# Meta tokens' squares load 16 columns, norm rows and key factors spread with all 128 rows, first attention's meta outputs four heads at once

## The reference

```
def rms_norm(x, g):
    y = xf * lax.rsqrt(jnp.mean(xf * xf, axis=-1, keepdims=True) + EPS)
    return (y * g.astype(jnp.float32)).astype(x.dtype)

# first attention: 8 query heads, 2 key and value heads of 128
q = rms_norm(q.reshape(B, Tp, N_HEADS, A_HEAD_DIM), gq)
k = rms_norm(k.reshape(B, Tp, A_KV_HEADS, A_HEAD_DIM), gk)
o = jnp.einsum('bqgrk,bqkgd->bqgrd', p, vsel)        # four query heads share one value head

# second attention: two maps of 8 heads of 64
q1 = rms_norm(q1.reshape(B, Tp, N_HEADS, B_HEAD_DIM), gq)
k1 = rms_norm(k1.reshape(B, Tp, N_HEADS, B_HEAD_DIM), kn_b)
```

## Time and profile before

| | |
|---|---|
| median of 3 runs | 1302.97 us (1302.85 to 1303.08) |
| span of the profiled execution, first to last instruction | 1300.2 us |
| what the median lies above that span | 2.8 us |
| TensorE matmuls busy | 1276.4 us, 98% |
| TensorE weight loads busy | 1183.3 us, 91% |
| VectorE busy | 980.0 us, 75% |
| ScalarE busy | 669.6 us, 51% |
| GpSimd busy | 494.2 us, 38% |

### The profile page before, as it was taken

How to read it: one execution, slowest core, us unless ns; L and a number is a source line. 1 busy time by engine, 2 the same in 40 slices (tenths; PEclk the granted TensorE clock), 3 DMA queues, 4 the chain that set the end, 5 groups by cost and what they waited for, 6 DMA issues and landing times.

```text
span 1300.2 us, 27004 instructions
## 1 busy us (share of the span) xinstructions
PE 1276.4 (98%) x8914; PEld 1183.3 (91%) x8914; DVE 980.0 (75%) x1567; ACT 669.6 (51%) x1103; POOL 494.2 (38%) x454
## 2 busy tenths in 40 slices
PE   8999999999999999999999999999999999999998
PEld 7999999999999989999888898888888988888887
DVE  5686899975656668999765687799866776999553
ACT  5545555554455555666544354455444565455442
POOL 1142455541212216555411033289611102799222
PEclk9999999999999999999999999999999999999999
DMA  8731556665633315666567555666666543666762
GB/s 218 156 98 50 155 170 180 175 176 165 183 110 110 102 34 166 191 189 182 163 196 235 156 166 159 187 186 191 197 193 190 147 136 89 179 193 189 204 190 82
DMA packets 403203, 209.20 MB, mean 161 GB/s; under 512 B 20552, under 2 KB 397680, under 8 KB 403104
## 3 DMA queue, kind: packets, MB, share of 16 engines
q1 hardware_dynamic: 402016, 205.37, 55.1%
q0 software_dynamic: 784, 2.51, 0.9%
q10 hardware_dynamic: 320, 0.21, 0.1%
HBM read 206.98 MB, written 1.27 MB: 160 GB/s over the span
## 4 chain that ended last, share of the span: by engine, by line
PE 90%; DVE 6%; issue 2%; POOL 1%; ACT 1%; DMA 0%; DVEq 0%; POOLq 0%; ACTq 0%
PE bank L621 22%; PE bank L615 15%; PE bank L617 14%; PE bank L616 14%; PE bank L622 12%; DVE w_lo L2083 2%; PE bank L764 1%; PE bank L1186 1%; PE bank L1188 1%; PE bank L1187 1%; PE bank L751 1%; PE bank L723 1%; PE bank L1038 1%; PE bank L1025 1%; PE bank L693 1%
## 5 line engine op out<-in xcount | busy, mean ns | idle before, releaser
L2083 DVE TENSOR_TENSOR w_lo<-w_raw,w_hi 128x1024 fp32r<-128x1024 f32 x391 | 514.6, 1329 | 28.7 <-ACT w_hi L1443 27.9
L1443 ACT ACTIVATE w_hi<-w_raw 128x1024 fp32r<-128x1024 f32 x391 | 410.6, 1052 | 130.8 <-PE bank L622 66.4
L615 PE MATMUL bank<-split_x,w_lo 128*128 128x272 f32 (+2 forms) x1128 | 329.2, 292 | 0.2 <-issue 0.2
L617 PE MATMUL bank<-split_x,w_hi 128*128 128x272 f32 (+2 forms) x1128 | 322.8, 286 | 0.0
L616 PE MATMUL bank<-split_x,w_hi 128*128 128x272 f32 (+2 forms) x1128 | 322.7, 286 | 0.0
L621 PE MATMUL bank<-split_w,w_hi 128*128 128x512 f32 x880 | 306.9, 392 | 0.7 <-POOL split_w L1942 0.5
L622 PE MATMUL bank<-split_w,w_lo 128*128 128x256 f32 x880 | 246.5, 280 | 0.0
L615 PEld LDWEIGHTS bank<-split_x,w_lo 128*128 128x128 f32 x1128 | 212.4, 188 | 2.8 <-issue 0.6
L616 PEld LDWEIGHTS bank<-split_x,w_hi 128*128 128x128 f32 x1128 | 212.5, 188 | 0.3
L617 PEld LDWEIGHTS bank<-split_x,w_hi 128*128 128x128 f32 x1128 | 212.4, 188 | 0.3
L621 PEld LDWEIGHTS bank<-split_w,w_hi 128*128 128x128 f32 x880 | 164.7, 187 | 37.8 <-POOL split_w L1942 0.8
(11 more groups left out here) (300 smaller groups left out, 1854.5 us busy)
## 6 DMA issues: line engine op xcount, KB each, us to landing
w_raw<-in_mlp_w_dram SPq DMA_DIRECT2D x256, 256.0 KB, 3.2
w_raw<-in_w_up_dram SPq DMA_DIRECT2D x176, 256.0 KB, 3.3
w_raw<-in_w_down_dram SPq DMA_DIRECT2D x64, 256.0 KB, 3.2
w_raw<-in_a_w_in_dram SPq DMA_DIRECT2D x64, 256.0 KB, 3.4
w_raw<-in_w_in_a_dram SPq DMA_DIRECT2D x32, 256.0 KB, 4.1
w_raw<-in_w_kv_b_dram SPq DMA_DIRECT2D x32, 256.0 KB, 3.2
w_raw<-in_a_w_out_dram SPq DMA_DIRECT2D x32, 256.0 KB, 3.2
w_raw<-in_w_down_dram SPq DMA_DIRECT2D x32, 192.0 KB, 3.8
```

Source lines behind the costliest of these rows:

```text
L615: pe.matmul(dst, lo, mov_h, start=first, stop=False)
L617: return pe.matmul(dst, hi, mov_h, start=False, stop=last)
L1443: act.activation(w_hi[:, n % R, :], w_raw[:, n % R, :], ACT.Copy)\
L2083: dve.tensor_tensor(w_lo[:, n % R, :], w_raw[:, n % R, :], w_hi[:, n % R, :].bitcast(F32), ALU.subtract)\
```

## The change

1. Sums of squares: for M only the 16 meta tokens' columns are loaded, and 16 rows of the sums are written. The two key heads of the first attention keep the 128 columns (`every_row`).
2. Spreads: for M all 128 rows of the factor's column are used with the first 16 columns of the identity. The tile of the array becomes 128 by 128 in `spread` and 128 by 64 in `spread_key`.
3. `meta_outputs` of the first attention makes two matmuls of 64 columns in place of eight of 16, since four heads share a value head. The second attention's stays.
4. VectorE: the factor buffer `fq_a` is set to 1.0 once at the start, and `query_sums` adds for M on 16 rows in place of 128.

```
             def spread(dst, column, tiles, off=0):
                 for tt in tiles:
                     lo, hi = TOK[tt]
-                    n = hi - lo
-                    ins = pe.matmul(dst[:, lo - off:hi - off],
-                                    column(tt)[0:n, :].to_broadcast([n, P]),
-                                    ident[0:n, 0:n], start=True, stop=True)
+                    ins = pe.matmul(dst[:, lo - off:hi - off], column(tt).to_broadcast([P, P]),
+                                    ident[:, 0:hi - lo], start=True, stop=True)
...
-            def head_squares(r0, slot, two, ssq_sem, sums=misc[2]):
+            def head_squares(r0, slot, ssq_sem, sums=misc[2], every_row=False):
...
-                    ins = pe.matmul(dst, u_ring[:, slot, lo:lo + P], rhs, start=True, stop=True)
+                    lo, hi = TOK[tt]
+                    n = P if every_row else hi - lo
+                    ins = pe.matmul(sums[0:n, 3 * r0 + TT[tt]:3 * r0 + TT[tt] + 1],
+                                    u_ring[:, slot, lo:lo + n], ones[:, 0:1], start=True, stop=True)
...
             def meta_outputs(att, v_of):
...
-                for hh in range(H):
-                    prob, val = pt_m[0:META, hh, :], v_of(hh, "M")[0:META, :]
-                    ins = pe.matmul(dst[:, META * hh:META * (hh + 1)], val, prob,
+                n = 4 if att.name == "a" else 1
+                for hh in range(0, H, n):
+                    prob, val = pt_m[0:META, hh:hh + n, :], v_of(hh, "M")[0:META, :]
+                    ins = pe.matmul(dst[:, META * hh:META * (hh + n)], val, prob,
                                     start=True, stop=True)
...
@@ spread_key
-                                        fac(fk_a, 2 * c + e, TT[tt])[0:n, :].to_broadcast([n, 64]),
-                                        ident[0:n, 0:n], start=True, stop=True)
+                                        fac(fk_a, 2 * c + e, TT[tt]).to_broadcast([P, 64]),
+                                        ident[:, 0:hi - lo], start=True, stop=True)
@@ squares_sums
-                    ins = pe.matmul(SUM_B[:, c0 + TT[tt]:c0 + TT[tt] + 4:3], sq_b[n % 2][:, lo:lo + P],
-                                    headcol, start=True, stop=True)
+                    ins = pe.matmul(SUM_B[0:hi - lo, c0 + TT[tt]:c0 + TT[tt] + 4:3],
+                                    sq_b[n % 2][:, lo:hi], headcol, start=True, stop=True)
...
+            dve.memset(fq_a, 1.0)
```

More of the change, by code:

```diff
@@ L701, in rb_sums @@
                     .then_inc(S["rb_sums"], 1)
-            def head_squares(r0, slot, two, ssq_sem, sums=misc[2]):
+            def head_squares(r0, slot, ssq_sem, sums=misc[2], every_row=False):
                 for tt in "ABM":
-                    lo = TOK[tt][0]
-                    if two:
-                        dst = sums[:, 3 * r0 + TT[tt]:3 * r0 + TT[tt] + 4:3]
-                        rhs = headcol
-                    else:
-                        dst = sums[:, 3 * r0 + TT[tt]:3 * r0 + TT[tt] + 1]
-                        rhs = ones[:, 0:1]
-                    ins = pe.matmul(dst, u_ring[:, slot, lo:lo + P], rhs, start=True, stop=True)
+                    lo, hi = TOK[tt]
+                    n = P if every_row else hi - lo
+                    ins = pe.matmul(sums[0:n, 3 * r0 + TT[tt]:3 * r0 + TT[tt] + 1],
+                                    u_ring[:, slot, lo:lo + n], ones[:, 0:1], start=True, stop=True)
                 ins.then_inc(ssq_sem, 1)
@@ L888, in _ @@
                         pe.wait_ge(a_sq, k + 1)
-                        head_squares(8 + k, k % 4, False, a_ssq)
+                        head_squares(8 + k, k % 4, a_ssq, every_row=True)
                 if g == 13:
@@ L915, in last_squares_a @@
                 pe.wait_ge(a_sq, 10)
-                head_squares(7, 9 % 4, False, a_ssq, misc[3])
+                head_squares(7, 9 % 4, a_ssq, misc[3])
                 pe.wait_ge(S["tile_read"], ST["in"].t0 + 18)
@@ L2384, in query_sums @@
                 for tt in "ABM":
-                    f = half_heads(att, fq_a, 4 * half, TT[tt])
-                    ins = dve.tensor_scalar(f, half_heads(att, misc[2 + half], 4 * half, TT[tt]),
-                                            e_scaled[:, TT[tt]:TT[tt] + 1], None, ALU.add)
+                    n = TOK[tt][1] - TOK[tt][0]
+                    f = half_heads(att, fq_a, 4 * half, TT[tt])[0:n]
+                    ins = dve.tensor_scalar(f, half_heads(att, misc[2 + half], 4 * half, TT[tt])[0:n],
+                                            e_scaled[0:n, TT[tt]:TT[tt] + 1], None, ALU.add)
                     if half == 1 or tt == "M":
```

5 lines of the change are left out of this document (2 added, 3 removed).

## The result

The changed kernel takes 1297.4 us (median of 9 runs, 1296.1 to 1300.1), the kernel before 1302.3 (9 runs, 1300.9 to 1303.1). The ratio is 0.9964 [0.9956, 0.9972]. Two of the 21 runs of the kernel before in that second comparison took 1757 and 1784 us at a mean granted clock of 0.67 and 0.65, and the ratio leaves them out. In all runs listed but one (2.8 us) the time is 1.8 or 1.9 us above its span (the profiled run of the changed kernel: 1296.1 and 1294.3).

The account below looks back on a forecast made before the run. TensorE, with a matmul in flight for 98% of the span, was the bound. Terms 1.2 + 0.58 + 0.9 + 1.3 - 0.1 = 3.9 us, less 0.1 for waits, gave 1302.97 - 3.8 = 1299.2 us; eight-in-ten range 1298.0 to 1302.0.

Parts of the forecast that it names:

- items 1, 2, 4: Four norm rows with M save 0.30 us each; the first attention's key factors save 0.58 us, its meta outputs 1.3.
- item 3: Second attention's key factors, eight times: no tile change between pairs with 128 rows, 0.11 us saved each, 0.9 in sum.
- item 5: Squares, 24 groups: two tile changes use up what M's 16-column loads save; 0.1 us lost in sum.
- The 24th group: Last squares of the first attention, followed by meta logits already of the 16-column tile: 0.16 us saved.
- Does it reach the end: Whether TensorE's savings shorten the whole program: nearly all pass, 3.8 of 3.9 us, including those around the first attention.
- The waits hang on TensorE's own logits and should not grow: First attention: TensorE's waits of 0.52 and 1.09 us stay, so the 1.0 us saved ahead passes; argued against the clock loss.
- signs of being wrong: Prediction wrong if squares' groups end over 0.05 us each from even, or if the first attention's waits change.
- rival B: Gains in and ahead of the first attention come back as waits; only 1.6 us saved, 1301.4 us; chance 16%.
- The base: The 1302.97 us median from which the saving was subtracted, taken as lying 2.8 us above the 1300.2 us span.
- The sum: Whole kernel: savings of all parts total 3.9 us, of which 3.8 us were taken off the time.
- later waits: 0.1 us of the 3.9 us saving was left to waits of a later engine.
- rival D: First attention: growing waits drop TensorE's clock to half, costing up to 11 us; 1303 us or more; chance 7%.

Follow-up runs that it names:

- e1_spreads: The kernel before with only the norm-row and key-factor spreads using all 128 rows for M; 1299.5 us, ratio 0.9975.
- e2_meta: The kernel before with only the first attention's meta outputs done four heads at once; 1301.15 us, ratio 0.9989.
- k65: The kernel before with M's norm rows and key factors spread from 65 rows instead of 16; 1300.5 us, ratio 0.9985.
- r_after: The changed kernel run again, unchanged, beside fresh runs of the kernel before (the second comparison); 1297.4 us, ratio 0.9963.
- f_before: The kernel before with 13 filler passes that wait for nothing in the second attention's end, block 12's outputs moved later; 1303.0 us, ratio 1.0015.
- f_after: The changed kernel with 13 filler passes that wait for nothing in the second attention's end, block 12's outputs moved later; 1298.8 us, ratio 0.9977.
- fill1_before: The kernel before with six filler passes ahead of turn_v(7) in the second attention's end; 1302.4 us, ratio 1.0.
- w_after: The changed kernel with 14 more filler passes in two TensorE waits of the second attention's end; 1303.2 us, ratio 1.0003.

## Why the prediction was off, point by point

The forecast was 1.8 us too long. In short, 0.65 us of that are the base to which the sum was added, 0.6 us the sum (4.4 us by the traces and not 3.8), and 0.5 us are in neither.

- **Norm rows, key factors of the first attention, meta outputs (items 1, 2, 4):** right, 0.29, 0.57 and 1.31 us against 0.30, 0.58 and 1.3. e1_spreads and e2_meta show that they reach the end.
- **Key factors of the second attention (item 3):** right in kind and mis-sized, 0.15 for 0.11 us each, 1.2 for 0.9 in sum. The step was "The first M pair follows after the 0.11 us of the pairs before it" with its end, "the second 0.06 later because little is moved, and the way back to the full array still has to be paid, the 0.16 to 0.22 of now": of the 0.33 to 0.42 that it gave, I took the upper end, and the measured saving means 0.38. The trace shows how they run: in k65, pairs of matmuls start every 0.11 us, the second M pair 0.03 us behind the first (the forecast had 0.06), and the next block 0.15 behind that (it had 0.16 to 0.22).
- **Squares (item 5):** right. The way in and the way out eat what the short load saves, to 6 ns in a group (686 for 680 ns). The forecast had 0.20, 0.02 and 0.12 us from the last full load on, the trace has 0.207, 0.015 and 0.118. The 24th group saved 0.18 us, where 0.16 was forecast. By the rule that a weight load takes its columns divided by 1.2 ns (the Trainium skill, "TensorE: Matmul & The Clock Gate", "LDWEIGHTS (loading the stationary operand)"), 65, 64 and 16 columns would take 54, 53 and 13 ns, which are estimates from the page. M's two loads start 59, 55 and 15 ns apart, so the trace agrees within 5 ns. But by the rule alone 64 columns would be as good as 65, and they cost 4.4 us more by the 24 groups. The Trainium skill, "TensorEngine Tiling (Array Packing)", "Key Properties", says that changing the tiling mode drains the engine, and gives no size. That fits what stands at 64 and 16 columns and not at 65: 0.10 us in, and 0.09 to 0.10 us out.
- **Does it reach the end:** yes, nearly. From 16 to 510 us the traces part by 4.2 us without the half clock, where the places of the table and the last group of squares give 4.4. "The waits hang on TensorE's own logits and should not grow" failed by 0.28 us (1.37 for 1.09), and so did "so all of it passes". A change of these waits was one of the forecast's own signs of being wrong, and it came. It is the small beginning of rival B, and no more.
- **The base, the step that failed first:** "The median lies 2.8 above the span, so 1302.97 - 3.8". In the listed runs time and span differ by 1.8 or 1.9 us (one has 2.8). The 1.0 more was the difference between one execution and three others, which I had taken for a fixed part of the program. The three runs also lay high: later medians of the kernel before are 1302.2 to 1302.4. With 1302.3 the same sum gives 1298.5, inside the range, and still 1.1 too long.
- **The sum, the second step:** 3.8 us, where three pairs of profiles give 4.4 to 4.5 once start, half clock and the passes from 803 to 838 us are set aside (before and after, before and r_after, f_before and f_after). 0.3 is item 3. 0.26 is the passes between 512 and 650 us, for which there was no term. 0.1 had been left to later waits.
- **The clock:** the half-clock stretch was treated only as a possible loss (rival D), priced at 1.7 us. It costs 1.1 us, it is in some executions and not in others of the same program, and it was in the profile of before and not in that of after (nor in those of e2_meta, fill1_before, f_before and f_after). The prediction had no term for an execution that comes out better.
- **The 0.5 us left:** the comparisons of medians gave 4.9 and 5.0 us, the traces give 4.4 to 4.5. The interval of the ratio (a difference of 3.6 to 5.7 us) holds both. Three things that go with the execution and not with the kernel are each as large as the rest: the slow start (up to 1.0 us), the half-clock stretch (1.1) and the passes from 803 to 838 us (0.7). Whether the changed kernel's runs had them more seldom is not settled, since only the mean clock is known of the runs without a profile, and it doesn't tell: e2_meta and fill1_before have 0.998 without a half-clock stretch, as others have with one.
- **What makes the clock fall:** open. The longest wait (2.1 us) was followed by the longest falls, but a wait of 1.55 us went by without one, and one program had the fall in one profile and not in the other, with the same waits of 0.85 and 1.06 us.
- **Range:** 1298.0 was too high by 1.9 us to hold the nine runs' lowest and by 0.6 for their median. It was made from the edits' bounds alone; the scatter of the base, over 2 us between runs of one kernel, had no place in it.

## What to carry to other kernels

Price a small matmul by the distance from its load's start to the next one's, and look for the places where the shape changes between 64 columns or fewer and 65 or more: two loads of 65 columns between full ones cost 0.11 us a group less than two of 128, and 0.19 less than two of 64, which have the way in and the way out. Between 16 rows and 65 it was the same (64 rows were not tried). If a narrow operand stands alone among full ones, widen it to 65 or to all 128 rather than cut it, as long as the extra rows or columns are harmless. Cut it only if a run of several of them shares the way in and out. All this is measured on float32 passes. Before adding a sum to a median, see how far single executions of the same kernel stand apart, and keep a term for it in the range, on both sides. When two traces are compared, take their distance stage by stage: what grows where nothing was edited is either the execution or an effect that nobody thought of, and a second profile of each kernel tells which.

## What was not expected of the hardware

- 65 columns are quicker than 64: the loads start 0.059 and 0.055 us apart, but with the ways in and out a group takes 0.57 us against 0.76. Over 24 groups that is 4.4 us, and the medians of two kernels that are otherwise the same are 4.8 us apart.
- At the program's start the passes of 272 columns followed each other at 0.227 us, the pace of the half clock, in twelve of the seventeen profiles, until the trace's first clock record (14.78 us in the kernel before, 15.56 in k65, 12.48 in w_after). In the five in which that record starts ahead of the first such pass (after, e1_spreads, f_before, f_after and fill1_before, 10.47 to 11.33 us) none was slow. It is worth up to 1.0 us in an execution and goes with no edit. A window's clock of 1.00 ahead of the first record says nothing.
- Passes at full clock have more than one pace. The stretch from 802 to 840 us took 37.9 or 38.6 us, by the execution, and that from 512 to 650 us 138.05 or 137.8, by the kernel.
- A filler that needs a bank still being read turned a wait of 1.05 us into one of 2.1 us; 13.7 us at half clock followed (6.8 in the kernel before), and the place took 7.8 us longer.
